# Diagonal and finest-level scores taken as channel sums, and two start-up slabs read in pairs

## The chip, the cores and the metric

The kernel runs on one core of one Trainium2 chip, as one launch. The metric is the device time of the launch in microseconds (us), the median of several runs. TensorE (PE in the profile) multiplies matrices, VectorE (DVE), ScalarE (ACT) and GpSimd (POOL) do the elementwise work, and SyncE (SP) issues nearly all DMAs. Each engine works through its own list of instructions in order, and semaphores are the only thing that holds one engine for another.

## The reference

One inference step of a one-layer decoder: 256 prompt tokens and 8 sample tokens share all weights, and everything is float32. A gated linear recurrence with twelve heads (eight HGRN2 heads with values 128 wide, four GLA heads with values 256 wide) stands between large projections.

```python
a = _rmsnorm(h, n_pre_mix)
z = einsum('bld,dn->bln', a, w_in)              # about 10,300 columns
o_h, s_h = _gated_recurrence(q_h, k_h, i_h, log_f, s_h0)
o_g, s_g = _gated_recurrence(q_g, k_g, v_g, log_a, s_g0)
merged = sigmoid(m_h) * (norm(o_h) * silu(zg) @ w_hgrn_up) + sigmoid(m_g) * (norm(o_g) * silu(gr) @ w_gla_up)
h = h + _rmsnorm(merged @ w_out, n_post_mix)
h = h + _rmsnorm(square(relu(_rmsnorm(h) @ w_ff1)) @ w_ff2, n_post_ffn)
h = h + sigmoid(h @ w_ple_gate) * (p_i @ w_ple)

# inside a block of the recurrence, b is the running sum of the log gates:
decay  = exp(where(causal, b[t] - b[s], -inf))
scores = einsum('bhtk,bhsk,bhtsk->bhts', q, k, decay)
o      = einsum('bhts,bhsv->bhtv', scores, v) + (q * exp(b)) @ state
```

For t = s the decay is 1, so that score is the sum over the 128 channels of q[t]·k[t].

## The kernel before, in words

Tokens lie along the free dimension (264 = 256 + 8), features along the 128 partitions. The weights lie in DRAM as tiles of 128 output features by 2048 inputs, in the order of use, and are read in halves, called slabs (128x1024, 512 KB), into a ring of four. A float32 product is made of three products in the rounded type fp32r: ACT rounds a slab (`round_slab`, line 355, raw to whi), DVE takes the remainder (`rest_slab`, line 360, wlo), and TensorE multiplies whi and wlo by the rounded activations and whi by their remainder (lines 380 to 382, 24 matmuls of 264 columns a slab). Each engine waits for the one ahead of it: SP for the remainder that frees a raw slot, ACT for the landing and for TensorE to have left the slot of whi, DVE for ACT, TensorE for DVE.

The first tile group (`T_RANK`) is eight tiles wide: for each of the 16 input blocks k, one slab holds this block of all eight tiles, 128 columns of each. Slabs k = 0 and 1 are read in two halves of four tiles each (lines 471 to 477), slabs 2 and on whole (line 348); all in pieces of 128 columns. Between them SP reads parts of the activations x.

The heads run in loops (first head alone, then heads 1 to 7, then 8 to 11), each over eight slabs of other projections, so that TensorE has work while the head's own chain passes through the other engines. On TensorE, after slab 4 of a head come: transposition of v (`turn_v`, line 757), the scores (`scores`, lines 761 to 771), transposition of the decayed keys (`turn_kd`, line 778); slabs 5 and 6; scores times v (`prob_v`, line 787) and the new state (line 795); slab 7, with the sum of squares for the head's norm in its middle (`head_norm`, lines 801 and 802 for the eight narrow heads, 805 for the four wide ones).

The scores are made by levels. Level 0 couples the two blocks of 128 tokens; level l = 1 to 7 couples the neighbouring halves of length 128 >> l, and the two diagonal blocks (line 766) hold the terms t = s. Each is a plain float32 matmul of 128 columns, which runs as two instructions. DVE makes the decays (`level_decays`), ACT takes their exponential, and DVE multiplies them by q and k (`level_operands`). After the scores DVE masks them from PSUM (lines 1581 and 1584) and adds the levels into three blocks, `pairs` (line 1592). Here `slab(n)` on DVE or ACT is the preparation of the slab that TensorE takes two later; on DVE the order after the last level is kd (1559), slab(4), slab(5), m_tile(1), slab(6), masks and additions, slab(7), m_tile(2), the first half of the next head's decays (1444 to 1447), then `sq_lo` (1603), the remainder of the squares that `head_norm` multiplies. POOL copies q and k of the next head (1937, 1939) once the scores of this head are done, and for the wide heads adds the squares of two tiles (1944).

Of the kernel before, what the change touches and what calls it, by code (L numbers as in the profile page):

```python
# [28 lines left out]
P = 128  # L29
# [72 lines left out]
def build(nc, t):  # L102
# [79 lines left out]
    with nc.sbuf_tensor("gate_w", [2 * RANK, GH * P], F32) as gate_w, nc.sbuf_tensor("rank_z", [2 * RANK, TOK], F32) as rank_z:  # L182
        pass
    S = sb("S", [P, 2, UNIT])
# [6 lines left out]
    with nc.sbuf_tensor("o_first", [P, TOK], F32), nc.sbuf_tensor("sq_lo", [P, NP_TOK], F32R) as sq_lo:  # L191
# [32 lines left out]
    first_landed = [sem(f"first_landed{k}") for k in range(HALVED)]  # L224
# [25 lines left out]
        "act": ["v_tok_ready", "lev_exp", "kd_exp", "kd_tok_ready", "sq_ready", "sq_rounded",  # L250
                "ln_rs", "rs_ready", "o_hi_done", "s_out_ready", "sg_abs", "sg_exp", "sg_ln", "sg_sigma"],
        "dve": ["sq_parted", "lev_sub", "lev_ready", "kd_ready", "masked", "probs_ready", "sg_ls",
# [63 lines left out]
    def lefts(ap, h):  # L316
        return cells(ap, h, 0, P + h, 2 * h)

# [22 lines left out]
    def load_wide(sp, T, k, tile, first=False):  # L341
# [3 lines left out]
        if not first:  # L345
            sp.wait_ge(lo_ready, 2 * T + (k - RING + 1))
# [14 lines left out]

    def rank_rest(dve, T, par, half, end, done):

        s = slot_of(par, half)
        hi = whi[:, s, 0:RANK].bitcast(F32)
        dve.tensor_tensor(whi[:, s, RANK:2 * RANK], raw[:, s, 0:RANK], hi, ALU.subtract)
        at = slice(P, end)
        dve.tensor_tensor(wlo[:, s, at], raw[:, s, at], whi[:, s, at].bitcast(F32), ALU.subtract).then_inc(done, 1)
# [95 lines left out]
    def _(sp):  # L464
# [6 lines left out]
        for k in range(HALVED):  # L471
            if k:
                load_x(k)
            for half, landed in enumerate((first_landed[k], slab_landed[k])):
                at = T_RANK + FIRST * half
                sp.dma_start(raw[:, k, part_of_first(half)].rearrange("p (n c) -> p n c", n=FIRST),
                             t["stream"][at:at + FIRST, :, k * P:(k + 1) * P].rearrange("n p c -> p n c")).then_inc(landed, 16)
        load_x(2)
        load_wide(sp, T_RANK, 2, T_RANK, first=True)
# [6 lines left out]
        for dst, name in ((masks, "masks"), (ident, "ident"), (head_gain, "head_gain"),  # L486
                          (gate_b, "gate_b")):
            sp.dma_start(dst[:], t[name]).then_inc(const_landed, 16)
        for part in range(2):
# [182 lines left out]
    def _(pe):  # L672
# [28 lines left out]
        pe.wait_ge(const_landed, 16 * 6)  # L701
# [59 lines left out]
        def scores(H, D):  # L761
            pe.wait_ge(h_sem["lev_ready"], now(H))
# [7 lines left out]
            pe.matmul(DG[:, P:2 * P], lev[:, 0, 1, :], lev[:, 0, 0, :], start=True, stop=True)\  # L770
              .then_inc(h_sem["scores_done"], 1)
# [9 lines left out]
        def prob_v(H, D):  # L781
# [3 lines left out]
            for d in range(D):  # L785
                v = slice(d * P, (d + 1) * P)
                pe.matmul(O[d][:, 0:2 * P], v_tok[:, 0, v], pairs[:, 0:2, :], start=True, stop=False, skip_group_check=True)  # L787
                mm = pe.matmul(O[d][:, P:2 * P], v_tok[:, 1, v], pairs[:, 2, :], start=False, stop=True, skip_group_check=True)  # L788
# [9 lines left out]
        def head_norm(H, D):  # L798
            if D == 1:
                pe.wait_ge(h_sem["sq_parted"], now(H))  # L800
# [6 lines left out]
        def head(H, D, first=False):  # L807
# [16 lines left out]
            turn_kd(H)  # L824
            slab(5)
# [111 lines left out]
    def _(act):  # L937
# [27 lines left out]
        for k in range(KT):  # L965
# [5 lines left out]
            if k < HALVED:  # L971
                act.wait_ge(first_landed[k], 16)
                act.copy(whi[:, k, part_of_first(0)], raw[:, k, part_of_first(0)]).then_inc(first_hi, 1)
                act.wait_ge(slab_landed[k], 16)
                act.copy(whi[:, k, part_of_first(1)], raw[:, k, part_of_first(1)]).then_inc(hi_ready, 1)
# [140 lines left out]
        def head(H, D, next_D, first=False):  # L1116
# [21 lines left out]
            slab(5)  # L1138
            slab(6)
            turned(H, D)  # L1140
# [10 lines left out]
            if D == 1:  # L1151
                act.wait_ge(h_sem["sq_ready"], now(H))
                act.copy(sq_hi[:], sq[:, 0, 0:NP_TOK]).then_inc(h_sem["sq_rounded"], 1)
# [173 lines left out]
    def _(dve):  # L1327
# [14 lines left out]
        for k in range(KT):  # L1342
# [5 lines left out]
            if k < HALVED:  # L1348
# [4 lines left out]
                dve.tensor_tensor(wlo[:, k, at], raw[:, k, at], whi[:, k, at].bitcast(F32), ALU.subtract)\  # L1353
# [133 lines left out]
        dve.wait_ge(const_landed, 16 * 6)  # L1487
# [27 lines left out]
        def head(H, D, more=True, opening=False):  # L1515
# [20 lines left out]
            def level_operands(l):  # L1536
# [16 lines left out]
            def last_levels():  # L1553
# [5 lines left out]
                dve.tensor_tensor(kd[:], kd[:], k_b[:, 0:NP_TOK], ALU.mult).then_inc(h_sem["kd_ready"], 1)  # L1559

# [10 lines left out]
            slab(4)  # L1571
            slab(5)
# [7 lines left out]
            for n, (first, last) in enumerate(((0, 4), (4, LEVELS - 1))):  # L1580
# [3 lines left out]
            dve.tensor_tensor(pairs[:], DG[:, 0:3 * P].rearrange("s (b t) -> s b t", b=3),  # L1584
                              ident[:].rearrange("s (b t) -> s b t", b=3), ALU.mult).then_inc(h_sem["masked"], 1)
            for l in range(1, LEVELS):
                h = HALF[l]
                to = cells(pairs[:, 0, :], h, h, 2 * P - h, 2 * h)
                of = packed(probs[:, l - 1, :], h)

                dve.wait_ge(h_sem["masked"], (LEVELS + 1) * H + (l + 3))
# [471 lines left out]
```

## Time and profile before

| | |
|---|---|
| median of 3 runs | 1628.47 us (1628.04 to 1629.47) |
| profiled execution, its own time | 1628.97 us |
| its span | 1627.2 us |
| PE busy | 1620.3 us (100%) in 13332 matmuls |
| DVE busy | 1109.9 us (68%) |
| ACT busy | 842.2 us (52%) |
| POOL busy | 181.7 us (11%) |
| DMA | 329.17 MB, mean 202 GB/s |
| granted TensorE clock | 1.00 throughout |

A matmul's duration in the trace (0.28 us for 264 columns) is its passage through the pipeline; the next one starts after about 0.12 us. What TensorE costs is therefore read from starts, not from durations. The heads lie between about 253 and 600 us of the span.

### The profile page before, as it was taken

Reading aid. Unit: us, or ns where it says so; the run is one execution under the profiler, and the core shown is the slowest. Engines: PE = TensorE matmul, PEld = TensorE weight load, DVE = VectorE, ACT = ScalarE, POOL = GpSimd, SP = SyncE. Lnnn points to the kernel's source line nnn. Section 1 sums busy time; section 2 is a strip of 40 time slices with the busy share of each in tenths; the row PEclk is TensorE's granted clock in tenths of the full one; section 3 lists DMA queues with packets and bytes.
Section 4 is the critical chain, followed back from the end, with each engine's and each line's share of the span. In section 5 each row is a group of like instructions: output and inputs, shape, how many; then the busy total and the mean of one; then the engine's idle time right before and its main releaser. Section 6 shows DMA issues by size and latency. Waiting matters only on the chain.

```text
span 1627.2 us, 35049 instructions
## 1 busy us (share of the span) xinstructions
PE 1620.3 (100%) x13332; PEld 1615.8 (99%) x13332; DVE 1109.9 (68%) x1917; ACT 842.2 (52%) x1192; POOL 181.7 (11%) x166
## 2 busy tenths in 40 slices
PE   9999999999999999999999999999999999999999
PEld 9999999999999999999999999999999999999999
DVE  7548767888888876655986665566555665555774
ACT  7575765666666665433654334443444334443452
POOL 3101000111111100055300000000000000035200
PEclk9999999999999999999999999999999999999999
DMA  9577895565555467755675865588557775555564
GB/s 274 161 230 225 267 270 174 164 191 162 192 166 181 155 206 229 270 181 185 173 214 186 247 207 180 188 259 243 174 181 242 245 222 185 181 197 181 167 192 144
DMA packets 151178, 329.17 MB, mean 202 GB/s; under 512 B 16944, under 2 KB 79536, under 8 KB 150608
## 3 DMA queue, kind: packets, MB, share of 16 engines
q1 hardware_dynamic: 143888, 326.00, 64.3%
q10 hardware_dynamic: 7232, 2.43, 0.6%
q8 instruction: 33, 0.54, 0.1%
q14 instruction: 25, 0.20, 0.0%
HBM read 310.08 MB, written 18.30 MB: 202 GB/s over the span
## 4 chain that ended last, share of the span: by engine, by line
PE 98%; DMA 1%; DVE 1%; ACT 0%; SPq 0%; issue 0%
PE bank L380 29%; PE bank L381 29%; PE bank L382 28%; PE bank L398 3%; PE bank L400 3%; PE bank L403 2%; PE bank L768 1%; DMA raw<-in_stream 1%; PE bank L795 0%; PE bank L787 0%; PE bank L766 0%; PE bank L788 0%; PE bank L757 0%; PE bank L732 0%; PE bank L770 0%; PE bank L778 0%
## 5 line engine op out<-in xcount | busy, mean ns | idle before, releaser
L355 ACT CAST whi<-raw 128x1024 fp32r<-128x1024 f32 x532 | 547.9, 1048 | 470.7 <-PE bank L382 388.5
L380 PE MATMUL bank<-a_hi,whi 128*128 128x264 f32 x2576 | 734.2, 285 | 0.1
L381 PE MATMUL bank<-a_hi,wlo 128*128 128x264 f32 x2576 | 729.7, 283 | 0.0
L382 PE MATMUL bank<-a_lo,whi 128*128 128x264 f32 x2576 | 729.4, 283 | 0.0
L360 DVE TENSOR_TENSOR wlo<-raw,whi 128x1024 fp32r<-128x1024 f32 x518 | 629.6, 1246 | 109.8 <-ACT whi L355 108.8
L380 PEld LDWEIGHTS bank<-a_hi,whi 128*128 128x128 f32 x2576 | 485.2, 188 | 0.8 <-issue 0.7
L381 PEld LDWEIGHTS bank<-a_hi,wlo 128*128 128x128 f32 x2576 | 485.5, 188 | 0.1
L382 PEld LDWEIGHTS bank<-a_lo,whi 128*128 128x128 f32 x2576 | 482.9, 187 | 0.0
L380 PE MATMUL bank<-b_hi,whi 128*128 128x264 f32 x1280 | 363.1, 284 | 0.0
L381 PE MATMUL bank<-b_hi,wlo 128*128 128x264 f32 x1280 | 362.6, 283 | 0.0
L382 PE MATMUL bank<-b_lo,whi 128*128 128x264 f32 x1280 | 362.4, 283 | 0.0
L381 PEld LDWEIGHTS bank<-b_hi,wlo 128*128 128x128 f32 x1280 | 241.2, 188 | 0.0
L380 PEld LDWEIGHTS bank<-b_hi,whi 128*128 128x128 f32 x1280 | 241.1, 188 | 0.0
L382 PEld LDWEIGHTS bank<-b_lo,whi 128*128 128x128 f32 x1280 | 239.9, 187 | 0.0
L1281 ACT ACTIVATE lev<-lev 128x264 f32<-128x264 f32 x64 | 27.2, 425 | 165.5 <-DVE lev L1777 165.5
L1690 DVE TENSOR_TENSOR room<-room,bank 128x264 f32<-128x264 f32 (+1 forms) x48 | 20.6, 429 | 106.9 <-PE bank L382 106.9
L1883 POOL TENSOR_TENSOR sq<-room 128x264 f32<-128x264 f32 x2 | 2.2, 1086 | 721.9 <-DVE room L1690 620.0
L398 PE MATMUL bank<-b_hi,whi 128*128 128x264 f32 x256 | 73.3, 286 | 0.3 <-DVE b_lo L1339 0.3
L403 PE MATMUL bank<-b_hi,wlo 128*128 128x264 f32 x256 | 72.8, 284 | 0.0
L400 PE MATMUL bank<-b_lo,whi 128*128 128x264 f32 x256 | 72.7, 284 | 0.0
L1783 DVE TENSOR_TENSOR a_lo<-lev,a_hi 128x264 f32 (+1 forms) x64 | 27.3, 432 | 63.8 <-ACT a_hi L1283 63.8
L1777 DVE SCALAR_TENSOR_TENSOR lev<-bank,r_bc 128x264 f32<-128x264 f32 x64 | 27.1, 432 | 52.6 <-PE bank L382 52.5
(222 smaller groups left out, 1497.7 us busy)
## 6 DMA issues: line engine op xcount, KB each, us to landing
raw<-in_stream SPq DMA_DIRECT2D x532, 512.0 KB, 4.7
m_spill<-stage SPq DMA_DIRECT2D x32, 132.0 KB, 3.7
lev<-m_spill SPq DMA_DIRECT2D x16, 264.0 KB, 2.8
room<-in_x SPq DMA_DIRECT2D x7, 528.0 KB, 7.8
S<-in_state_hgrn SPq DMA_DIRECT2D x6, 512.0 KB, 6.7
out_new_hgrn_sample<-S SPq DMA_DIRECT2D x6, 512.0 KB, 6.8
S<-in_state_gla SPq DMA_DIRECT2D x5, 512.0 KB, 6.7
out_new_gla_sample<-S SPq DMA_DIRECT2D x5, 512.0 KB, 7.5
```

Source lines behind the costliest of these rows:

```text
L355: act.copy(whi[:, s, :], raw[:, s, :]).then_inc(hi_ready, 1)
L360: dve.tensor_tensor(wlo[:, s, :], raw[:, s, :], whi[:, s, :].bitcast(F32), ALU.subtract).then_inc(lo_ready, 1)
L380: pe.matmul(out, whi[:, s, w], hi[:, k0 + k, :], start=start and k == 0, stop=False)
L381: pe.matmul(out, wlo[:, s, w], hi[:, k0 + k, :], start=False, stop=False)
L382: mm = pe.matmul(out, whi[:, s, w], lo[:, k0 + k, :], start=False, stop=stop and k == HT - 1)
L398: pe.matmul(out, whi[:, s, w], hi[:, k, :], start=k == 0, stop=False, skip_group_check=True)
L400: mm = pe.matmul(out, whi[:, s, w], lo[:, k, :], start=False, stop=rank and k == KT - 1, skip_group_check=True)
L403: return pe.matmul(out, wlo[:, s, w], hi[:, k, :], start=False, stop=k == KT - 1, skip_group_check=True)
L1281: act.activation(u, u, ACT.Square).then_inc(u_ready, 1)
L1690: ins = dve.tensor_tensor(out, out, MM[par][:, 0:TOK], ALU.add)
L1777: dve.scalar_tensor_tensor(out=u, in0=bank[:, 0:TOK], scalar=0.0, in1=r_bc[:], op0=ALU.max, op1=ALU.mult).then_inc(tiles_drained, 1)
L1783: dve.tensor_tensor(a_lo[:, T - T0, :], u, a_hi[:, T - T0, :].bitcast(F32), ALU.subtract).then_inc(a_lo_ready, 1)
```

## The change

In each head the two diagonal matmuls and the one of level 7 go. Instead three rows of products are summed over the channels by TensorE with a matrix of ones: q·k of the two blocks, made on POOL (`dots_of`), and the product of the two operands of level 7, made on DVE, in a tile `dots` of 384 columns. ACT rounds it to `dots_hi`, DVE takes the remainder `dots_lo`, and two fp32r matmuls of 384 columns (`sum_dots`) follow the transposition of kd. ACT copies v and rounds `dots` ahead of its slab(6); DVE moves slab(6) behind the masks and additions. The mask of the last level becomes an instruction of its own. At the start, slabs 1 and 2 of the first tile group are read together: four tiles of both in one DMA, in pieces of 256 columns (1024 bytes), then the other four; the second part of x follows them. `ident` is read in three DMAs with its blocks in another order.

```diff
@@ sync: first loads
-        for k in range(HALVED):
-            if k:
-                load_x(k)
-            for half, landed in enumerate((first_landed[k], slab_landed[k])):
-                at = T_RANK + FIRST * half
-                sp.dma_start(raw[:, k, part_of_first(half)]..., t["stream"][at:at + FIRST, :, k * P:(k + 1) * P]...)
+        for half, landed in enumerate((first_landed, slab_landed[0])):
+            at = T_RANK + FIRST * half
+            sp.dma_start(by_block(raw[:, 0, part_of_first(half)]), t["stream"][at:at + FIRST, :, 0:P]...).then_inc(landed, 16)
+        load_x(1)
+        for half in range(2):
+            at = T_RANK + FIRST * half
+            sp.dma_start(raw[:, 1 + half, :]..., t["stream"][at:at + FIRST, :, P:3 * P]...).then_inc(slab_landed[1 + half], 16)
         load_x(2)
-        load_wide(sp, T_RANK, 2, T_RANK, first=True)
         load_wide(sp, T_RANK, 3, T_RANK, first=True)
@@ load_wide
-            sp.wait_ge(lo_ready, 2 * T + (k - RING + 1))
+            sp.wait_ge(lo_ready, 2 * T + (k - RING + (2 if T == T_RANK and k == RING + 1 else 1)))
@@ tensor: scores
-            for B in range(2):
-                at = slice(B * P, (B + 1) * P)
-                pe.matmul(DG[:, 2 * B * P:(2 * B + 1) * P], k_b[:, at], q_b[:, at], start=True, stop=True)
-            for l in range(1, LEVELS):
+            for l in range(1, LEVELS - 1):
...
+        def sum_dots(H, D):
+            pe.wait_ge(h_sem["parts_ready"], dots_now(H, D))
+            pe.matmul(DG[:, 0:3 * P], ones_r[:], dots_hi[:], start=True, stop=False)
+            pe.matmul(DG[:, 0:3 * P], ones_r[:], dots_lo[:], start=False, stop=True).then_inc(h_sem["scores_done"], 1)
@@ tensor: head
             turn_kd(H)
+            sum_dots(H, D)
             slab(5)
@@ scalar: head
             slab(5)
+            turned(H, D)
+            act.wait_ge(h_sem["kq_ready"], second_now(H))
+            act.wait_ge(h_sem["lev_ready"], second_now(H))
+            act.copy(dots_hi[:], dots[:]).then_inc(h_sem["parts_rounded"], 1)
             slab(6)
-            turned(H, D)
@@ vector: last_levels
+                dve.wait_ge(h_sem["lev_ready"], first_now(H))
+                dve.tensor_tensor(dots[:, 0:P], lev[:, LEVELS - 1, 0, :], lev[:, LEVELS - 1, 1, :], ALU.mult)
@@ vector: head
             slab(4)
+            dve.wait_ge(h_sem["parts_rounded"], dots_now(H, D))
+            dve.tensor_tensor(dots_lo[:], dots[:], dots_hi[:].bitcast(F32), ALU.subtract).then_inc(h_sem["parts_ready"], 1)
             slab(5)
...
-            slab(6)
             dve.wait_ge(h_sem["scores_done"], now(H))
...
+            dve.tensor_tensor(probs[:, LEVELS - 2, :], DG[:, 0:P], both[:, LEVELS - 2, :], ALU.mult).then_inc(h_sem["masked"], 1)
...
+            slab(6)
@@ gpsimd
+        def dots_of(H):
+            pool.wait_ge(h_sem["kq_ready"], first_now(H))
+            pool.tensor_tensor(turned_blocks(dots), q_b[:, 0:NP_TOK]..., k_b[:, 0:NP_TOK]..., ALU.mult).then_inc(h_sem["kq_ready"], 1)
```

On TensorE, in the loop of heads 1 to 7, the stretch from the transposition of v to slab 5 was:

```order
L757 MATMUL bank<-ident,v_st 128x128
L762 REGISTER_ALU
L766 MATMUL bank<-q_b,k_b 128x128 [waits ln_rs,lev_ready]
L766 MATMUL bank<-q_b,k_b 128x128
L768 MATMUL bank<-lev,k_lev 128x128 x7
L770 MATMUL bank<-lev 128x128
L778 MATMUL bank<-ident,kd 128x128 [waits v_tok_ready,kd_ready]
```

The same stretch is now the following, with other line numbers (797 for 768, 811 for 778):

```order
L789 MATMUL bank<-ident,v_st 128x128
L794 ISA
L797 MATMUL bank<-lev,k_lev 128x128 [waits ln_rs,lev_ready]
L797 MATMUL bank<-lev,k_lev 128x128 x5
L799 MATMUL bank<-lev 128x128
L808 REGISTER_ALU
L811 MATMUL bank<-ident,kd 128x128 [waits v_tok_ready,kd_ready]
L811 MATMUL bank<-ident,kd 128x128
L803 MATMUL bank<-dots_hi,ones_r 128x384 [waits parts_ready]
L804 MATMUL bank<-dots_lo,ones_r 128x384
```

Three float32 matmuls are gone, and two of 384 columns stand behind the transposition of kd with a wait of their own.

On DVE, in the same loop, from kd to the mask of the diagonal blocks, before (L360 is the remainder of a slab, L1373 the drain m_tile(1)):

```order
L1559 TENSOR_TENSOR kd<-kd,k_b 128x256 [waits kd_exp]
L359 ISA
L360 TENSOR_TENSOR wlo<-raw,whi 128x1024 [waits hi_ready]
L359 REGISTER_ALU
L360 TENSOR_TENSOR wlo<-raw,whi 128x1024 [waits hi_ready]
L1373 TENSOR_TENSOR stage<-bank,r_bc 128x264 [waits slabs_multiplied]
L359 ISA
L360 TENSOR_TENSOR wlo<-raw,whi 128x1024 [waits hi_ready]
L1579 REGISTER_ALU [waits scores_done]
L1581 TENSOR_TENSOR probs<-bank,both 128x512 [waits pv_done]
L1581 TENSOR_TENSOR probs<-bank,both 128x384
L1584 TENSOR_TENSOR pairs<-bank,ident 128x384
```

And now (L380 is the remainder, L1412 the drain):

```order
L1600 TENSOR_TENSOR kd<-kd,k_b 128x256 [waits kd_exp]
L1602 TENSOR_TENSOR dots<-lev 128x128 [waits lev_ready]
L380 TENSOR_TENSOR wlo<-raw,whi 128x1024 [waits hi_ready]
L1616 TENSOR_TENSOR dots_lo<-dots,dots_hi 128x384 [waits parts_rounded]
L379 REGISTER_ALU
L380 TENSOR_TENSOR wlo<-raw,whi 128x1024 [waits hi_ready]
L1412 TENSOR_TENSOR stage<-bank,r_bc 128x264 [waits slabs_multiplied]
L1623 REGISTER_ALU [waits scores_done]
L1625 TENSOR_TENSOR probs<-bank,both 128x512 [waits pv_done]
L1625 TENSOR_TENSOR probs<-bank,both 128x256
L1628 TENSOR_TENSOR probs<-bank,both 128x128
L1629 TENSOR_TENSOR pairs<-bank,ident 128x384
```

`dots` and `dots_lo` have come in, the third remainder has moved behind the additions, and the second mask is in two pieces.

On SP, the first loads were (in_x are parts of x, in_stream are slabs):

```order
L476 DMA raw<-in_stream 128x4x128 x2
L467 DMA room<-in_x 128x264
L476 DMA raw<-in_stream 128x4x128 x2
L467 DMA room<-in_x 128x528
L348 DMA raw<-in_stream 128x8x128 x2
```

They are now:

```order
L503 DMA raw<-in_stream 128x4x128 x2
L497 DMA room<-in_x 128x264
L508 DMA raw<-in_stream 128x4x256 x2
L497 DMA room<-in_x 128x528
L368 DMA raw<-in_stream 128x8x128
```

Slab 2 has moved ahead of the part of x that holds k = 2 and 3, and the halves of slab 1 come with those of slab 2.

## Rows read from the trace of the kernel before

**Rows 1.** The page's chain of work that ended last, shares of the span.
```profile
PE 98%; DMA 1%; DVE 1%; ACT 0%; SPq 0%; issue 0%
```

**Rows 2.** Timeline of PE in head 3: start, duration, engine, line, operation, count.
```profile
349.84 0.38 PE L757 MATMUL bank<-ident,v_st 128*128 128x128 f32 x2
350.06 0.61 PE L766 MATMUL bank<-q_b,k_b 128*128 128x128 f32 x4
350.51 1.73 PE L768 MATMUL bank<-lev,k_lev 128*128 128x128 f32 x14
352.30 0.38 PE L778 MATMUL bank<-ident,kd 128*128 128x128 f32 x2
...
361.58 0.28 PE L801 MATMUL bank<-sq_hi,ones_r 128*128 128x256 f32 x1
361.70 0.28 PE L802 MATMUL bank<-sq_lo,ones_r 128*128 128x256 f32 x1
```

**Rows 3.** Timeline of DVE in head 3, from kd to sq_lo.
```profile
349.43 0.41 DVE L1559 TENSOR_TENSOR kd<-kd,k_b 128x256 f32<-128x256 f32 x1
349.77 2.35 DVE L360 TENSOR_TENSOR wlo<-raw,whi 128x1024 fp32r<-128x1024 f32 x2
...
358.80 0.28 DVE L1444 TENSOR_TENSOR lev<-cum 128x128 f32<-128x128 f32 x1
...
360.41 0.42 DVE L1603 TENSOR_TENSOR sq_lo<-sq,sq_hi 128x256 fp32r<-128x256 f32 x1
```

**Rows 4.** Timeline of ACT in head 3.
```profile
351.00 0.37 ACT L1096 COPY v_tok<-bank 128x256 f32<-128x256 f32 x1
```

**Rows 5.** Timeline of DVE in the first tile group.
```profile
8.84 0.55 DVE L368 TENSOR_TENSOR wlo<-raw,whi 128x384 fp32r<-128x384 f32 x1
9.31 0.68 DVE L1353 TENSOR_TENSOR wlo<-raw,whi 128x512 fp32r<-128x512 f32 x1
...
12.78 1.08 DVE L368 TENSOR_TENSOR wlo<-raw,whi 128x896 fp32r<-128x896 f32 x1
```

**Rows 6.** Timeline of PE in the first tile group; brackets: idle time, releaser.
```profile
14.01 0.36 PE L398 MATMUL bank<-a_hi,whi 128*128 128x264 f32 x1 [0.91 <-DVE wlo L368]
...
23.00 0.36 PE L398 MATMUL bank<-a_hi,whi 128*128 128x264 f32 x1 [0.23 <-DVE wlo L368]
```

**Rows 7.** Timeline of ACT in the first tile group.
```profile
8.60 0.62 ACT L975 CAST whi<-raw 128x512 fp32r<-128x512 f32 x1
...
9.84 0.89 ACT L969 ACTIVATE a_hi<-room,gains 128x128 fp32r<-128x128 f32 x3 [0.29 <-DMA room<-in_x]
11.61 1.05 ACT L355 CAST whi<-raw 128x1024 fp32r<-128x1024 f32 x1 [0.88 <-DMA raw<-in_stream]
```

**Rows 8.** Timeline of PE in head 9 (a wide head).
```profile
514.58 0.60 PE L757 MATMUL bank<-ident,v_st 128*128 128x128 f32 x4
515.03 0.38 PE L766 MATMUL bank<-q_b,k_b 128*128 128x128 f32 x1
...
527.01 0.59 PE L805 MATMUL bank<-sq,ones 128*128 128x256 f32 x2
```

**Rows 9.** Timeline of DVE in head 9.
```profile
514.89 0.42 DVE L1559 TENSOR_TENSOR kd<-kd,k_b 128x256 f32<-128x256 f32 x1
```

**Rows 10.** What PE waited for ahead of line 766: releaser, us, times.
```profile
  DVE k_lev L1544: 0.2, 1
```

**Rows 11.** Timeline of PE between heads 0 and 1.
```profile
285.99 0.28 PE L382 MATMUL bank<-a_lo,whi 128*128 128x264 f32 x1
286.38 0.38 PE L380 MATMUL bank<-a_hi,whi 128*128 128x264 f32 x1
```

**Rows 12.** Timeline of POOL: the squares of head 9, and a product during two remainders.
```profile
525.64 0.91 POOL L1944 TENSOR_TENSOR sq<-sq 128x256 f32<-128x256 f32 x1 [5.99 <-ACT sq L1149]
...
691.69 1.54 POOL L1885 TENSOR_TENSOR sq<-room 128x264 f32<-128x264 f32 x1 [5.17 <-DVE room L1692]
```

**Rows 13.** Timeline of DVE during that product.
```profile
691.52 2.78 DVE L360 TENSOR_TENSOR wlo<-raw,whi 128x1024 fp32r<-128x1024 f32 x2
```

More of the change, by code:

```diff
@@ L183, in build @@
         pass
+    with nc.sbuf_tensor("dots", [P, 3 * P], F32) as dots, nc.sbuf_tensor("dots_hi", [P, 3 * P], F32R) as dots_hi, \
+         nc.sbuf_tensor("dots_lo", [P, 3 * P], F32R) as dots_lo:
+        pass
     S = sb("S", [P, 2, UNIT])
@@ L223, in build @@
     gains_landed = sem("gains_landed")
-    first_landed = [sem(f"first_landed{k}") for k in range(HALVED)]
+    first_landed = sem("first_landed")
     first_hi, first_lo = sem("first_hi"), sem("first_lo")
@@ L307, in before, with dots_now, first_now, second_now @@
         return H + 1
+    def dots_now(H, D):
+        return 2 * H + 2 if D == 1 else H + (HH + 2)
+    def first_now(H):
+        return 2 * H + 2
+    def second_now(H):
+        return 2 * H + 3
     def cells(ap, h, at, step, pitch):
@@ L317, in lefts, with turned_blocks @@
         return cells(ap, h, 0, P + h, 2 * h)
+    def turned_blocks(dots):
+        ap = dots[:, 2 * P:3 * P]
+        return bass.AP(ap.tensor, ap.offset, [list(ap.ap[0]), [-P, 2], [1, P]])
     def packed(ap, h):
@@ L360, in rest_slab, with by_block, first_rows @@
         dve.tensor_tensor(wlo[:, s, :], raw[:, s, :], whi[:, s, :].bitcast(F32), ALU.subtract).then_inc(lo_ready, 1)
+    def by_block(ap):
+        return ap.rearrange("p (n c) -> p n c", c=P)
+    def first_rows(k):
+        if k in (1, 2):
+            return raw[:, 1:3, :].rearrange("p s (n b c) -> p (s n) b c", n=FIRST, b=2)[:, :, k - 1, :]
+        return by_block(raw[:, k % RING, :])
     def rank_rest(dve, T, par, half, end, done):
-        s = slot_of(par, half)
+        s, k = slot_of(par, half), 2 * T + half
         hi = whi[:, s, 0:RANK].bitcast(F32)
-        dve.tensor_tensor(whi[:, s, RANK:2 * RANK], raw[:, s, 0:RANK], hi, ALU.subtract)
+        dve.tensor_tensor(whi[:, s, RANK:2 * RANK], first_rows(k)[:, 0, 0:RANK], hi, ALU.subtract)
         at = slice(P, end)
-        dve.tensor_tensor(wlo[:, s, at], raw[:, s, at], whi[:, s, at].bitcast(F32), ALU.subtract).then_inc(done, 1)
+        dve.tensor_tensor(by_block(wlo[:, s, at]), first_rows(k)[:, 1:end // P, :], by_block(whi[:, s, at].bitcast(F32)), ALU.subtract)\
+           .then_inc(done, 1)
     def multiply(pe, T, par, half, out, hi, lo, k0, start, stop, before_k=None, midway=None, at=HT // 2):
@@ L485, in _ @@
                 load_x(4 + (k - RING) // 3)
-        for dst, name in ((masks, "masks"), (ident, "ident"), (head_gain, "head_gain"),
-                          (gate_b, "gate_b")):
+        for dst, name in ((masks, "masks"), (head_gain, "head_gain"), (gate_b, "gate_b")):
             sp.dma_start(dst[:], t[name]).then_inc(const_landed, 16)
+        for to, of in ((0, 0), (1, 2), (2, 1)):
+            sp.dma_start(ident[:, to * P:(to + 1) * P], t["ident"][:, of * P:(of + 1) * P]).then_inc(const_landed, 16)
         for part in range(2):
@@ L799, in head_norm @@
             if D == 1:
-                pe.wait_ge(h_sem["sq_parted"], now(H))
+                pe.wait_ge(h_sem["parts_ready"], second_now(H))
                 pe.matmul(DG[:, 0:NP_TOK], ones_r[:], sq_hi[:], start=True, stop=False)
@@ L1601, in head @@
             if D == 1:
-                dve.wait_ge(h_sem["sq_rounded"], now(H))
-                dve.tensor_tensor(sq_lo[:], sq[:, 0, 0:NP_TOK], sq_hi[:].bitcast(F32), ALU.subtract).then_inc(h_sem["sq_parted"], 1)
+                dve.wait_ge(h_sem["parts_rounded"], second_now(H))
+                dve.tensor_tensor(sq_lo[:], sq[:, 0, 0:NP_TOK], sq_hi[:].bitcast(F32), ALU.subtract).then_inc(h_sem["parts_ready"], 1)
             slab(8)
@@ L1956, in _ @@
         pool.tensor_copy(by_head(s_cols[:, 3, :, :]), gates[:, :, at]).then_inc(cols_ready, 1)
+        pool.wait_ge(units_summed, HEADS)
+        with pool.Fori(0, 1) as H:
+            dots_of(H)
         with pool.Fori(1, HH) as H:
             head(H, 1)
+            dots_of(H)
         with pool.Fori(HH, HH + 1) as H:
             head(H, 2)
+            dots_of(H)
         with pool.Fori(HH, HEADS - 1) as H:
             head(H + 1, 2)
+            dots_of(H + 1)
             add_halves(H)
```

54 lines of the change are left out of this document (31 added, 23 removed).

## The prediction

> **What bounds the kernel now.** I read the page's chain of waits first: 98% of the span is TensorE, one matmul behind another [rows 1]. So an edit counts only by what it does to TensorE's list: work taken out of it, put into it, or a wait. The list of waits by engine names no stall of TensorE in the heads longer than 0.2 us, so I went on to the timelines of a steady narrow head (head 3), engine by engine, with t = 0 at the first transposition of v, 349.84 [rows 2], and looked for how early each partner is. All times below are after that zero.
>
> TensorE: scores from 0.22, kd's transposition at 2.46, head_norm at 11.74 [rows 2]. DVE begins kd at -0.41 and then shows no idle time down to sq_lo, which ends at 10.99 [rows 3]: all these 11 us it is one unbroken list. TensorE starts a matmul 0.15 us after the end of the remainder it waited for (12.78 + 1.08 = 13.86 against 14.01) [rows 5, 6]. DVE is thus 11.74 - 10.99 - 0.15 = 0.60 us early for head_norm, and the change puts work into just this stretch.
>
> **The change, part by part.** *Matmuls.* From 350.51 to 352.30 pass 14 instructions of line 768 and the two of line 770: 1.79 / 16 = 0.112 us each [rows 2]. Six go per head (two diagonals and level 7, two instructions each): 0.67 us. Two fp32r matmuls of 384 columns come in. The trace has 256 columns, 0.12 us from start to start [rows 2]. Between 0.12 (no dearer) and 0.18 (in proportion to the columns) I take 0.17, near proportion, since most of the 0.12 is columns. That adds 0.34. Net -0.33 us a head, -4.0 us for twelve, if nothing waits. The Trainium skill (TensorE: Matmul & The Clock Gate, section Back-to-back issue gap) gives a gap that grows with the columns plus a few ns; by it a matmul would be 0.16 us and the gain 0.2 us larger in all.
>
> *DVE's list* grows by three things: dots, 128 columns, 0.20 (eight such instructions between 358.80 and 360.41) [rows 3]; dots_lo, 384 columns, 0.47 (8.84 to 9.31) [rows 5]; the mask cut in two, another start, about 0.07 (what 0.20 for 128 and 0.47 for 384 columns leave for no columns). Together 0.74 us. slab(6) only changes places within the list, between kd and sq_lo both before and now, and frees nothing there. Behind dots_lo stand slab(5), m_tile(1), the masks and all the rest.
>
> *Where that ends.* If DVE starts where it does now, sq_lo comes 0.74 later and TensorE asks for it 0.33 earlier: 1.07 less the 0.60 in hand, a stall of 0.47 at head_norm. A stall gives DVE a longer lead into the next head, but the lead can't be used, since dots_lo waits for ACT: the transpositions end at 0.38 [rows 2], ACT's copy of v takes 0.37 [rows 4], of which the next instruction overlaps some 0.1, and the rounding of 384 columns about 0.5 (512 columns took 0.62 [rows 7]). So dots_hi ends near 1.21 and dots_lo starts near 1.24. From the end of the first remainder of rows 3 (1.14, half of 2.35 less the overlap) to the end of sq_lo DVE needs 10.99 - (-0.07) - 1.14 = 9.92; with dots_lo and the cut mask 10.46. That is 11.70, plus 0.15 for the hand-over 11.85, against TensorE at 11.41: a stall of 0.44. The two ways agree; I take 0.45. The first matmul after a wait took 0.36 instead of 0.28 [rows 2, 6], so 0.08 more. The wait of sum_dots itself costs nothing here: dots_lo ends at 1.79, seen at 1.94, and TensorE arrives at 2.46 - 0.67 + 0.13 = 1.92. A steady narrow head is then -0.33 + 0.45 + 0.08 = +0.20; heads 0 and 2 to 7: +1.4.
>
> *Between heads 0 and 1* TensorE has a gap of 0.39 instead of 0.12 [rows 11], behind a chain that starts at scores times v of head 0; a stall ahead of it is absorbed there: -0.27.
>
> *Late heads.* In head 9 DVE starts kd 0.31 after TensorE's transpositions begin, 0.72 later than in head 3 [rows 8, 9]. There kd 0.34, dots 0.20 and the remainder 1.14 put dots_lo at 1.99, its end at 2.54, seen at 2.69. TensorE, starting scores at 0.45 [rows 8], is there at 0.45 + 14 x 0.112 + 0.14 = 2.16: a stall of 0.53, and +0.20 net. Heads 10 and 11 look the same in the trace. The wide heads have no sq_lo. +0.6 for three. Head 8 is early, but its copy of v is twice as wide: a stall of about 0.2, -0.1 net. Head 1 is the one in which TensorE waited for DVE's last level [rows 10]: a late head that also has sq_lo, +0.6.
>
> *POOL's product* lies behind the copies of q and k for the next head, 20 us before it is wanted. While it runs DVE masks from PSUM. I cost it at nothing; if DVE were held by it, about 0.4 us a head would come on top (the hold in rows 13).
>
> *Start.* The pair lands before the second part of x. ACT met slab 1 already there at 8.60, x at 9.84 and slab 2 at 11.61 [rows 7]: 512 KB in about 1.77 us. Without faster pieces slab 1's second half comes near 10.4, x not after 11.6, ACT reaches slab 2 about 0.9 later and TensorE starts it at 14.9 instead of 14.01 [rows 6]. If pieces of 1024 bytes save a fifth of 3.5 us for the pair, it is 14.2. The second wait, 23.00, is behind a slab that comes after all these bytes and not later than before; it ends the start-up either way, and swallows a delay of up to about 0.4 us. I take -0.1, between -0.5 and +0.5. The three reads of ident and SP's two more issues, at 29 us, stand in a stretch where nothing on TensorE waits.
>
> Sum: 1.4 - 0.27 + 0.6 - 0.1 + 0.6 - 0.1 = +2.1 us. Against the profiled execution, 1628.97, that is 1631.1; the median of the runs is 0.5 lower, so the forecast is **1630.6 us**.
>
> **Rivals.** *No stalls: the gain is whole.* -4.0 - 0.1 gives 1624.4 us. For it: no listed wait in the heads now, and DVE has idle time in other stretches. Against: the 0.60 us at head_norm is measured, and 1.07 goes into it. *Half stalls*, where dots and dots_lo cost DVE or ACT less than the nearest rows say, or TensorE resumes faster: 0.2 us instead of 0.53 in seven heads, -2.3, near 1628 us. *POOL's squares are shut out (slower).* In the wide heads head_norm waits for POOL's sum of squares (line 1944), 525.64 in head 9, 11.06 after its zero, needed at 12.43 [rows 8, 12]. DVE now runs the next head's decays from about 10.4 to 12.1 and slab(8) straight behind them to 13.3. If POOL can't get in between, its sum ends near 13.9, and TensorE, due at 12.6, stands 1.4 us, in heads 8 to 10 (the last has no decays): +4.3, 1635 us. It decides as soon as slab(8) is ready before the decays end, which by my times is so by 0.1 us. Against it: at 691.69 POOL's product came during one remainder and was done before the second [rows 12], and the two together took 2.78 instead of 2.35 [rows 3, 13], so POOL got in between them at DVE's cost. By the Trainium skill (SBUF — State Buffer, section Who interferes with whom) a DVE instruction with two SBUF inputs and a POOL read contend, and the one issued first holds the port to its end; by that POOL waits one instruction and this rival falls. The rows just named agree, 0.43 us.
>
> **How the numbers follow.** The forecast has 0.52, its own range 1628.9 to 1632.9 (0.15 us up or down in ten heads, the start). Half stalls 0.22, no stalls 0.11, POOL shut out 0.15. No change that this measurement can tell is 0.2%, 1625.2 to 1631.7. Faster: the first rival, 0.11. Slower: the last rival and a fifth of the forecast's chance, 0.26. Within: 0.63. The range for 8 in 10, 1626.5 to 1634.0, leaves out most of the two outer rivals.
>
> **What would show it.** In the new profile: matmuls of 384 columns 0.16 to 0.18 us apart, and six fewer of 0.11; TensorE waiting for sq_lo at head_norm in the narrow heads by 0.3 to 0.6 us, DVE's list unbroken from dots_lo to sq_lo; sum_dots waiting for dots_lo in heads 1 and 9 to 11 by about 0.5 and hardly in heads 2 to 7; POOL's squares done before line 805's matmuls are due. At the start the wait for slab 2 shifts, and the sixth slab still starts near 23. Wrong would be: no wait at head_norm (then it is faster), stalls over 1 us in the wide heads (then slower), or a start-up that ends later than 23.5.

## The result, and the profile after

The changed kernel takes 1633.03 us (median of 12 runs, 1632.24 to 1636.41), the one before 1628.72 us beside it (12 runs, 1628.04 to 1629.47). The ratio is 1.0029, 95% interval 1.0021 to 1.0036: slower by 0.29%, 4.3 us. That lies inside the range (1626.5 to 1634.0) and 2.4 us above the forecast of 1630.6; the case thought likeliest, no change that can be told, did not come, since the whole interval is above 0.2%.

The page's first line of busy times and its chain of waits, to be held against [rows 1]:

```profile
PE 1620.2 (99%) x13284; PEld 1612.3 (99%) x13284; DVE 1120.7 (69%) x1953; ACT 848.0 (52%) x1204; POOL 181.3 (11%) x178
PE 89%; DVE 5%; issue 3%; ACT 1%; DMA 1%; POOL 1%; SPq 0%; DVEq 0%; ACTq 0%; POOLq 0%
```

TensorE has 48 matmuls less, and the span is 4.2 us longer (1631.4 against 1627.2): no work was added to TensorE, it waits. For what, the list of waits says (engine, line, releaser: us in total, times, longest; the two rows left out, of 1.7 and 0.3 us, are in the kernel before too). Of the rows shown, the kernel before has only the first kind:

```profile
PE bank L398 <- DVE wlo L368: 1.1, 2, 0.9
```

The changed kernel:

```profile
PE bank L428 <- DVE wlo L397: 2.4, 2, 1.5
...
PE bank L834 <- DVE sq_lo L1649: 1.3, 7, 0.2
PE bank L838 <- POOL sq L1996: 1.3, 1, 1.3
...
PE bank L803 <- DVE dots_lo L1616: 0.2, 1, 0.2
```

The first is the start-up, the second the norm of the narrow heads, the third the norm of a wide head, the fourth `sum_dots`. The next table is made from starts of matmuls in the two traces, in us: for each head the start of its first transposition of v, and the period to the next head's.

```
head   start before/after   period before/after  more   forecast
0      265.08  266.11       30.107  30.180      +0.07   -0.07 (with the gap behind it)
1      295.18  296.29       27.447  27.987      +0.54   +0.6
2..7   322.63  324.27       27.207  27.346      +0.14   +0.20   (each; six heads)
8      485.88  488.34       28.700  29.014      +0.31   -0.1
9      514.58  517.35       28.827  30.333      +1.51   +0.20
10     543.40  547.68       28.814  29.014      +0.20   +0.20
11     572.22  576.70       (to its norm)       -0.31   +0.20
```

Head 0 starts 1.03 late, the start-up's share (forecast -0.1). The heads add 3.14 (forecast 2.2). Behind them nothing is gained or lost.

**The start-up.** ACT's timeline (start, duration, instruction, in brackets the idle time before it and its releaser), then TensorE's; they answer to [rows 6, 7]:

```profile
9.96 0.62 ACT L1007 CAST whi<-raw 128x512 fp32r<-128x512 f32 x1 [1.74 <-DMA raw<-in_stream]
11.46 0.62 ACT L1009 CAST whi<-raw 128x512 fp32r<-128x512 f32 x1 [0.88 <-DMA raw<-in_stream]
...
13.09 1.03 ACT L1011 CAST whi<-raw 128x1024 fp32r<-128x1024 f32 x1
```

```profile
11.40 0.36 PE L428 MATMUL bank<-a_hi,whi 128*128 128x264 f32 x1 [1.55 <-DVE wlo L397]
...
15.48 0.36 PE L428 MATMUL bank<-a_hi,whi 128*128 128x264 f32 x1 [0.89 <-DVE wlo L397]
```

Slab 1's second half, rounded at 8.60 before, is in at 11.46. Slab 2 came with it, but ACT reaches its rounding only at 13.09, behind that half and the next part of x. TensorE stands twice before 16 us, and slab 2, the third slab, starts at 15.48 instead of 14.01. The wait that ended at 23.00 before is gone and gives 0.4 back.

**A steady narrow head.** TensorE at `sum_dots` and at the norm in head 3 (its zero is 351.62), then DVE; they answer to [rows 2, 3]:

```profile
353.40 0.38 PE L811 MATMUL bank<-ident,kd 128*128 128x128 f32 x2
353.54 0.42 PE L803 MATMUL bank<-dots_hi,ones_r 128*128 128x384 f32 x1
353.80 0.34 PE L804 MATMUL bank<-dots_lo,ones_r 128*128 128x384 f32 x1
353.98 0.28 PE L410 MATMUL bank<-a_hi,whi 128*128 128x264 f32 x1
354.09 0.28 PE L411 MATMUL bank<-a_hi,wlo 128*128 128x264 f32 x1
...
362.93 0.29 PE L412 MATMUL bank<-a_lo,whi 128*128 128x264 f32 x1
363.39 0.39 PE L834 MATMUL bank<-sq_hi,ones_r 128*128 128x256 f32 x1 [0.17 <-DVE sq_lo L1649]
363.61 0.28 PE L835 MATMUL bank<-sq_lo,ones_r 128*128 128x256 f32 x1
```

```profile
352.85 0.56 DVE L1616 TENSOR_TENSOR dots_lo<-dots,dots_hi 128x384 fp32r<-128x384 f32 x1 [0.33 <-ACT dots_hi L1178]
...
362.91 0.42 DVE L1649 TENSOR_TENSOR sq_lo<-sq,sq_hi 128x256 fp32r<-128x256 f32 x1
```

`sum_dots` does not wait. The norm starts 0.46 after the matmul ahead of it instead of 0.12 and its second matmul 0.22 after the first instead of 0.12: 0.34 of waiting and 0.10 of starting again.

**A wide head.** Head 9 on POOL, DVE and TensorE (the POOL row of before is in [rows 12], the norm in [rows 8]):

```profile
528.40 2.74 POOL L1996 TENSOR_TENSOR sq<-sq 128x256 f32<-128x256 f32 x1 [6.00 <-ACT sq L1188]
```

```profile
528.93 0.28 DVE L1485 TENSOR_TENSOR lev<-cum 128x128 f32<-128x128 f32 x1
529.13 0.29 DVE L1486 TENSOR_TENSOR lev<-cum 128x128 f32<-128x128 f32 x1
529.34 1.22 DVE L380 TENSOR_TENSOR wlo<-raw,whi 128x1024 fp32r<-128x1024 f32 x1
```

```profile
531.19 0.70 PE L838 MATMUL bank<-sq,ones 128*128 128x256 f32 x2 [1.26 <-POOL sq L1996]
```

POOL's sum of the squares, 0.91 us before, takes 2.74: it is asked for amid DVE's decays, which follow each other without a gap, and the remainder of slab(8) starts before the last of them has ended. It ends 0.58 after that remainder, and TensorE has stood 1.4 us. In heads 8 and 10 the same sum takes 1.60:

```profile
499.21 1.60 POOL L1996 TENSOR_TENSOR sq<-sq 128x256 f32<-128x256 f32 x1 [6.01 <-ACT sq L1188]
...
558.55 1.60 POOL L1996 TENSOR_TENSOR sq<-sq 128x256 f32<-128x256 f32 x1 [6.01 <-ACT sq L1188]
...
587.48 0.74 POOL L1996 TENSOR_TENSOR sq<-sq 128x256 f32<-128x256 f32 x1 [27.33 <-ACT sq L1188]
```

There it got through before the remainder was done (which took 1.75 instead of 1.22), and TensorE lost 0.27 by waiting and 0.10 by starting again. Head 11, without decays, takes 0.74.

### The profile page after: what moved, and what is told of

It reads as the page before. It is cut to its first block, busy times and chain, and to the rows that moved or that the text cites. A ratio compares the mean times of both kernels' runs of the same rounds, so it can differ in the third digit from the quotient of the medians.

```text
span 1631.4 us, 35080 instructions
## 1 busy us (share of the span) xinstructions
PE 1620.2 (99%) x13284; PEld 1612.3 (99%) x13284; DVE 1120.7 (69%) x1953; ACT 848.0 (52%) x1204; POOL 181.3 (11%) x178
## 4 chain that ended last, share of the span: by engine, by line
PE 89%; DVE 5%; issue 3%; ACT 1%; DMA 1%; POOL 1%; SPq 0%; DVEq 0%; ACTq 0%; POOLq 0%
PE bank L411 26%; PE bank L410 26%; PE bank L412 26%; PE bank L428 3%; PE bank L430 3%; PE bank L433 3%; DVE wlo L380 1%; DMA raw<-in_stream 1%; DVE pairs L1637 1%; DVE probs L1625 0%; POOL sq L1996 0%; ACT whi L375 0%; DVE lev L1485 0%; DVE lev L1486 0%; PE bank L797 0%
## 5 line engine op out<-in xcount | busy, mean ns | idle before, releaser
L380 DVE TENSOR_TENSOR wlo<-raw,whi 128x1024 fp32r<-128x1024 f32 x518 | 631.4, 1250 | 101.4 <-ACT whi L375 100.1
```

The source lines that it names most:

```text
L380: dve.tensor_tensor(wlo[:, s, :], raw[:, s, :], whi[:, s, :].bitcast(F32), ALU.subtract).then_inc(lo_ready, 1)
```

## The experiments

Each kernel was timed in five rounds beside the kernel before on the same chip; all ratios are to it.

**Start-up of before (heads_only).** The changed kernel with the old loads:

```diff
+        for k in range(HALVED):
+            if k:
+                load_x(k)
+            for half, landed in enumerate((first_landed[k], slab_landed[k])):
...
         load_x(2)
+        load_wide(sp, T_RANK, 2, T_RANK, first=True)
```

> The changed kernel with the start-up loads of the kernel before (slabs 1 and 2 apart, the second part of x ahead of slab 2); the heads are the changed ones. Theory: the paired start-up costs 1.0 us, as the two profiles have it (the gates' matmuls at 61.6 instead of 60.6), because slab 1's second half lands behind slab 2's first: 1632.0 us, 1.0 less than the changed kernel; the first wait ends near 14.0 again and the sixth slab's near 23.0. Rival: the 1.0 us is chance in when the first loads arrive (the first product started 0.4 us apart in the two profiles): 1633.0 us.

1631.33 us, ratio 1.0020 (1.0010 to 1.0029), 1.5 us less than the change by the ratios. All head periods from head 1 on are those of the changed kernel within 0.02 us; head 0's is 0.37 shorter, since `sum_dots` does not wait there. The wait for slab 2 ends at 13.80, and none follows.

**Pair alone (start_only).** The reverse, the paired loads in the kernel before:

```diff
+        load_x(1)
+        for half in range(2):
+            at = T_RANK + FIRST * half
+            sp.dma_start(raw[:, 1 + half, :]..., t["stream"][at:at + FIRST, :, P:3 * P]...)
         load_x(2)
-        load_wide(sp, T_RANK, 2, T_RANK, first=True)
```

> The kernel before with the paired start-up alone; its heads are those of before. Theory: the pair costs what its removal gave back, ratio 1.0020 instead of 1.0029, some 1.4 us, whatever the heads are: 1629.6 us, ratio 1.0008; head 0 starts near 266 instead of 265.1. Rival: the delay is taken up before the heads, by waits that the kernel before has anyway: ratio 1.000.

1629.60 us, ratio 1.0008 (0.9999 to 1.0017); its trace has the two waits, at 11.37 (1.70 us) and 15.45 (0.89), and every head starts 1.0 late with an unchanged period. Over all profiles here, head 0 starts at 265.41 to 266.25 in five kernels with the pair in 1024-byte pieces and at 264.21 to 265.24 in four with the old loads, 1.2 us apart in the mean, and the two groups do not overlap. So the pair costs 1.0 to 1.5 us, whatever the heads are; that it costs anything is shown by the profiles, since the interval of start_only alone reaches no change.

**Pieces of 512 bytes (packets_512).** The order of the pair, not its pieces:

```diff
-            sp.dma_start(raw[:, 1 + half, :]..., t["stream"][at:at + FIRST, :, P:3 * P]...)
+            for k in (1, 2):
+                sp.dma_start(raw[:, 1 + half, :]...[:, :, k - 1, :], t["stream"][at:at + FIRST, :, k * P:(k + 1) * P]...)
```

> The changed kernel with the pair of slabs read in the same order and into the same places, but in four transfers with pieces of 512 bytes instead of two with pieces of 1024. Theory: the order alone (half of slab 2 ahead of slab 1's second half) makes the start-up late and the size of the pieces does nothing: 1633.0 us, the third slab near 15.5. Rival: pieces of 1024 bytes do save time, a fifth of the pair's 3.5 us, and the order's cost is larger than it looks: about 0.7 us later at the third slab, 1633.7 us.

1633.09 us, ratio 1.0028 (1.0018 to 1.0039): the time of the change, but in the profile it is made up otherwise. ACT's rounding of slab 1's second half and of slab 2, TensorE's start on slab 2, and its wait for POOL:

```profile
10.41 0.62 ACT L1010 CAST whi<-raw 128x512 fp32r<-128x512 f32 x1 [1.14 <-DMA raw<-in_stream]
...
12.04 1.03 ACT L1012 CAST whi<-raw 128x1024 fp32r<-128x1024 f32 x1
```

```profile
14.43 0.36 PE L428 MATMUL bank<-a_hi,whi 128*128 128x264 f32 x1 [0.89 <-DVE wlo L397]
```

```profile
PE bank L839 <- POOL sq L1997: 2.5, 2, 1.3
```

Slab 2 starts at 14.43, where the five kernels with large pieces have 14.78 to 15.48, and head 0 at 265.05, below all five (265.41 to 266.25) and among those with the old loads. The same total comes about because POOL holds up heads 9 and 10 here (periods +1.51 and +1.35 against before), where the change's profile has head 9 alone (head 10 +0.20). So neither theory is borne out, and the equal times do not show that the order makes the whole cost: in this one profiled execution head 0 starts 0.4 to 1.2 us earlier than with large pieces in the same order. How the cost divides between the order and the pieces stays open.

**Slab 2 ahead of x, without the pair (x_behind).** The kernel before with two lines exchanged:

```diff
-        load_x(2)
         load_wide(sp, T_RANK, 2, T_RANK, first=True)
+        load_x(2)
```

> The kernel before with one thing of the paired start-up: slab 2 is read ahead of the second part of x, in pieces of 512 bytes; slab 1 is not joined with it. Theory: the start-up's cost is that slab 1's second half waits for the first half of slab 2 (the wait of 1.97 us at the second slab); without the pair this wait isn't there, x comes some 1.8 us later than before, slab 2 starts near 14.9 instead of 14.0, and the wait near 22.5 takes up half of that: +0.4 us, ratio 1.0002. Rival: x behind slab 2 is the whole cost (the third slab waits for ACT, which waits for x), as much as with the pair: ratio 1.0008.

1630.25 us, ratio 1.0007 (0.9998 to 1.0016), as much as the pair by the ratio; but it does not tell the theories apart, since something else came in. TensorE's wait for slab 2 is one of 1.89 us, the third slab starts at 14.26 (0.25 later than before, less than either theory had), and no later wait is left; yet head 0 starts 1.33 late. The table by windows (stretch, its length, PE busy and matmuls, granted clock, DMA share, GB/s) shows why:

```profile
12.00:14.00 2.00, 0.37 (x4) 1.00 1.08 344
14.00:16.00 2.00, 1.74 (x13) 0.89 1.09 351
16.00:18.00 2.00, 2.00 (x11) 0.50 1.16 311
18.00:20.00 2.00, 2.00 (x14) 0.76 1.19 295
```

Behind that single wait the granted clock fell to half, 1.2 GHz, and came back before 20 us: 1.33 - 0.25 + 0.4 (the later wait that is gone) = some 1.5 us. In the profiles of the changed kernel and of the pair alone, where the idle time comes in two parts of 1.55 to 1.70 and 0.89 us, the clock is 1.00 in these stretches. Of the eleven timed runs of x_behind five have a mean clock of 0.999 (median 1630.55 us) and six 1.000 (median 1629.29, 0.8 above before), so the fall does not come every time. What x's place alone costs stays open.

**sq_lo ahead of the decays (sq_early).**

```diff
+            if D == 1:
+                dve.wait_ge(h_sem["parts_rounded"], second_now(H))
+                dve.tensor_tensor(sq_lo[:], sq[:, 0, 0:NP_TOK], ...)
             if more:
                 dve.wait_ge(h_sem["cum_ready"], now(H + 1))
                 level_half(0)
-            if D == 1:
...
```

> The changed kernel with sq_lo, the remainder that the narrow heads' norm waits for, ahead of the next head's first decays on DVE instead of behind them. Theory: TensorE waits at the norm because DVE's list ahead of sq_lo grew by 0.7 us, while its input has been ready for 1.4 us: the wait goes in heads 1 to 7, 0.37 us each, 2.6 us in all, near 1630.4 us, and a narrow head's period falls from 27.34 to 26.98. Rival 1: the input from ACT is what comes late, and nothing changes (1633.0). Rival 2: the decays, now 0.4 us later, delay the next head, and the wait comes back at sum_dots or at the scores: 1632 to 1633 us.

1629.47 us, ratio 1.0004 (0.9995 to 1.0013). The wait is gone in all seven heads, and a steady period is 26.90 instead of 27.35, 0.31 shorter than before the change (forecast 26.98; the 0.10 of starting again goes with the wait). Head 3:

```profile
360.68 0.42 DVE L1646 TENSOR_TENSOR sq_lo<-sq,sq_hi 128x256 fp32r<-128x256 f32 x1
```

```profile
362.10 0.29 PE L412 MATMUL bank<-a_lo,whi 128*128 128x264 f32 x1
362.22 0.28 PE L834 MATMUL bank<-sq_hi,ones_r 128*128 128x256 f32 x1
362.34 0.28 PE L835 MATMUL bank<-sq_lo,ones_r 128*128 128x256 f32 x1
```

The first theory holds; the decays, 0.4 later, delay nobody in heads 1 to 6, and head 7 by 0.1. In this profile heads 9 and 10 both wait 1.4 us for POOL, where the change's own had that in head 9 alone; the profiled execution, 1631.28 us, is the slowest of the eleven.

**Decays behind slab(8) in the wide heads (wide_order).**

```diff
-            if more:
+            if more and D == 1:
                 dve.wait_ge(h_sem["cum_ready"], now(H + 1))
                 level_half(0)
...
             slab(8)
+            if more and D == 2:
+                dve.wait_ge(h_sem["cum_ready"], now(H + 1))
+                level_half(0)
```

> The changed kernel with, in the wide heads 8 to 11, the next head's first decays behind slab(8) on DVE instead of ahead of it, which leaves DVE idle for about 1.4 us when the squares of the head come. Theory: POOL's sum of squares (1.60, 2.74 and 1.60 us in heads 8 to 10, 0.74 in head 11 that has no decays) is held out by DVE's decays and the remainder right behind them; without them it takes 0.74 to 0.9 us, and the waits at the norm go: 0.37 + 1.51 + 0.37 us less, near 1630.8 us. Rival: POOL's sum is long for another reason (its two inputs in one tile, ACT's reads), the waits stay: 1633.0 us. A second rival: the decays, 1.3 us later, make ACT's exponential and the next head's scores late: slower than 1633 us.

1630.78 us, ratio 1.0018 (1.0009 to 1.0027). POOL's sum in head 9, and where DVE's remainder now stands:

```profile
526.95 0.75 POOL L1999 TENSOR_TENSOR sq<-sq 128x256 f32<-128x256 f32 x1 [5.54 <-ACT sq L1188]
```

```profile
527.84 1.23 DVE L380 TENSOR_TENSOR wlo<-raw,whi 128x1024 fp32r<-128x1024 f32 x1 [1.47 <-ACT whi L375]
528.98 0.28 DVE L1483 TENSOR_TENSOR lev<-cum 128x128 f32<-128x128 f32 x1
```

The sum takes 0.75 us in all four wide heads, and the norm waits in none; heads 8 and 9 are 0.37 and 1.49 shorter. Of this 0.2 to 0.3 comes back in heads 10 and 11, where `sum_dots` waits again for `dots_lo`: the stall of head 9 had given DVE a lead.

**Diagonals alone (diag_only).** Level 7 stays a matmul of its own:

```diff
-            for l in range(1, LEVELS - 1):
+            for l in range(1, LEVELS):
...
-            pe.matmul(DG[:, 0:3 * P], ones_r[:], dots_hi[:], start=True, stop=False)
+            pe.matmul(DG[:, P:3 * P], ones_r[:], dots_hi[:, P:3 * P], start=True, stop=False)
```

> The changed kernel with level 7 as before: its matmul with the other levels, its mask with theirs, no product of it on DVE. Only the two diagonal blocks are summed over the channels (256 columns), and the rest of the change, paired start-up too, stays. Theory: the wait at the norm in the narrow heads is DVE's added 0.74 us less the 0.60 in hand and the matmuls saved; here DVE gets only 0.34 (256 columns) and TensorE loses four matmuls of 0.112 for two of some 0.14: sq_lo is 0.1 early, the wait is gone, a narrow head is 0.17 shorter than before, and with the start-up's 1.4 us the whole is near that of before, 1628.5, ratio 1.000. Rival: the wait comes from ACT's detour (the copy of v and the rounding ahead of its slab(6), which is there in both), and stays: ratio 1.002.

1629.47 us, ratio 1.0006 (0.9997 to 1.0015), between the theory's 1.000 and the rival's 1.002. In heads 2, 4, 6 and 7 the norm no longer waits and the period is 0.15 to 0.18 shorter than before; in heads 3 and 5 it waits 0.12 and the period is 0.03 to 0.04 longer; head 1 waits 0.24. This fits the length of DVE's list, to within a tenth. By itself it does not clear ACT's detour, which is shorter too (it rounds 256 columns instead of 384); sq_early does, where ACT's detour is that of the change and the wait is gone all the same. What I had not expected of it is POOL: its sum takes 1.44, 2.79 and 1.44 us in heads 8 to 10, and head 9 stands 1.5 us, with the smaller change too.

**The three corrections together (best), and without level 7 (best_diag).** The edits of heads_only, sq_early and wide_order in one kernel; then those of diag_only as well.

> The changed heads with three things put right: the start-up loads of the kernel before, sq_lo ahead of the next head's decays in the narrow heads, and in the wide heads the decays behind slab(8). Theory: the three costs are apart from each other, so the head periods of the single runs add up: against the kernel before -0.3 in head 0, +0.05 in head 1, -0.31 in each of heads 2 to 6, -0.2 in head 7, about 0 in heads 8 to 11, no start-up cost: -2.0 us, ratio 0.9988 (1626.2 us where the kernel before has 1628.2). Rival: DVE's list has no slack left, what is moved back delays the next head's scores or sum_dots, and half of it is lost: ratio 0.9995.

> The corrected version (start-up of before, sq_lo early, decays behind slab(8) in wide heads) with level 7 left as before, so that only the diagonal blocks are channel sums. Theory: a narrow head saves 4 x 0.112 - 2 x 0.12 = 0.21 us instead of 0.31, but in the late heads 1 and 9 to 11 sum_dots no longer waits for dots_lo, which is 0.1 us shorter with two instructions less in front of it, worth 0.25 to 0.3 us each: -0.2 in eight heads, -0.25 in four, -2.6 us in all against -2.0 for the version with level 7; ratio 0.9984. Rival: what the late heads win at sum_dots they wait at the next hand-over (the drains on DVE): -1.8 us, ratio 0.9989, not better than the version with level 7.

best: 1626.57 us, ratio 0.9991 (0.9982 to 1.0000). The periods of its heads 0 to 10 add up to -2.0 us against before, as forecast: -0.27, +0.02, five times -0.31, -0.24, and within 0.06 of nothing in heads 8 to 10. The saving of the wide heads is lost at `sum_dots`, which waits there for `dots_lo`. best_diag: 1625.88 us, ratio 0.9984 (0.9975 to 0.9993), faster than both kernels. All its heads are 0.17 to 0.25 shorter than before, 2.4 us in all against the 2.6 forecast, and of TensorE's waits only those of the start-up and one of 0.3 us behind the heads, which all kernels have, are left:

```profile
PE bank L724 <- POOL eps_col L1913: 1.7, 1, 1.7
PE bank L426 <- DVE wlo L395: 1.1, 1, 1.1
PE bank L426 <- DVE b_lo L1372: 0.3, 1, 0.3
```

That it beats best is likely but not shown: 0.7 us in the medians, on two chips, and the intervals overlap. It gains per late head what best loses, 0.2, and loses 0.1 per narrow head.

## Why the prediction was right and where it was wrong

**The start-up was mis-sized, with the wrong sign: -0.1 forecast, +1.0 in the profile, 1.3 to 1.5 by the timed pairs of kernels.** The step that failed is "slab 1's second half comes near 10.4"; it came at 11.46, where half of slab 2 goes with its first half, ahead of it. That this order alone makes it late is not shown: with pieces of 512 bytes in the same order the half was rounded at 10.41, as forecast (packets_512, one profile). ACT's serial list made it worse: the half, a part of x, and only then slab 2, 1.48 us later than before and not 0.9. And the second wait was not an end that swallows a delay: it was 0.39 long, gave that back, and went. By 1.47 - 0.39 = 1.08 the profile's 1.03 is accounted for. I had written that a start-up ending later than 23.5 would prove me wrong; the sixth slab, by which I dated that end, starts at 24.08 instead of 23.00, so by its own sign this part was wrong; TensorE's last wait of the start-up now ends at 15.48.

**POOL's squares were shut out in one head of three.** I had this as a rival (0.15, 1.4 us in each of heads 8 to 10), with the right place and price. I gave it little because the rows of two remainders [rows 12, 13] showed POOL getting in between them. In head 9 it did not get in between decays and remainder, in heads 8 and 10 it did; the decays ended 1.0 us after it was asked for. The forecast had put all three heads on one side, and the condition that I gave the rival, slab(8) ready before the decays end, did not divide them either: the rounding ended 0.15 to 0.17 us before the last decay did in all three. With the page cited there (the Trainium skill, SBUF — State Buffer, section Who interferes with whom), by which the first issued holds the shared port to its end, POOL would have waited one decay of 0.28 us; here it waited for five in a row, the running one and four more, and in head 9 for the remainder too. The rule names the two engines rightly; that POOL gets in at the next boundary was my reading of it, and in an unbroken row it did not. wide_order shows that DVE's unbroken row is the cause. So it is not semaphores alone that hold one engine for another, as the section on the chip has it: no semaphore stands between this sum and the decays.

**The narrow heads were right, step by step.** Matmuls: from the transposition of kd to the second matmul of slab 5 pass 354.09 - 353.40 = 0.69 us; in the kernel before 0.34:

```profile
352.30 0.38 PE L778 MATMUL bank<-ident,kd 128*128 128x128 f32 x2
352.43 0.37 PE L380 MATMUL bank<-a_hi,whi 128*128 128x264 f32 x1
352.64 0.28 PE L381 MATMUL bank<-a_hi,wlo 128*128 128x264 f32 x1
```

So two matmuls of 384 columns cost 0.35, as priced (0.34), and the first fp32r matmul behind a float32 one costs 0.08 to 0.09 more in both kernels. The page cited there (the Trainium skill, TensorE: Matmul & The Clock Gate, section Back-to-back issue gap) would have 0.16 for one by itself; 353.80 to 353.98 is 0.18, and the measurement decides. Without stalls the period fell by 0.31 (sq_early), forecast 0.33. DVE: `dots_lo` starts 1.23 after the head's zero (forecast 1.24), and `sq_lo` ends at 11.71 (11.70). Only the hand-over was smaller: the norm starts 0.06 after `sq_lo` ends, not 0.15, so the wait was 0.34 instead of 0.45, and a steady head cost 0.14 instead of 0.20.

**The late heads were right in kind.** Head 1 +0.54 (0.6). Head 9 waits about 0.4 at `sum_dots` (0.53), heads 8, 10 and 11 about 0.2; 10 and 11 less than forecast, because of the lead that head 9's stall gave DVE (without that stall, in wide_order, both wait 0.34). Head 10's +0.20 is the forecast's by luck: 0.2 at `sum_dots` and 0.37 at the norm stand there for 0.53 at `sum_dots`. The gap between heads 0 and 1 did not take up anything (0.39 still): head 0's norm did not wait, so nothing was there to take up. In head 0 `sum_dots` waited 0.34 in the changed kernel's profile and not at all in those of heads_only and wide_order; why is open.

In sum, forecast +2.1 and measured +4.2 in the profiles: start-up +1.1, head 9 +1.3, head 8 +0.4, head 0 +0.1; against that heads 2 to 7 -0.4, head 11 -0.5, head 1 -0.1. The two terms that were wrong, the start-up and POOL's sum in heads 8 and 9, come to +2.9 and the others to -0.8; the time lies in the range because the range was wide enough to hold both misses.

## What to carry to other kernels

Work that leaves a saturated engine lands on another one's list: before moving it, find in that list the instruction that the first engine waits for next, and put that one ahead of what nobody wants yet (here `sq_lo` ahead of the decays, 0.45 us a head). When two transfers are joined, ask when the earlier slab's last byte comes, and not when the pair is done. A gap in DVE's list can be the time in which POOL's instruction gets through (0.75 us in wide_order, 1.60 or 2.74 without the gap); where such a gap goes, count that instruction as late.

## What the runs showed of the hardware

- POOL's sum of 256 columns took 0.74 us with DVE idle, 1.44 to 1.60 when it had to wait for a row of DVE decays, and 2.74 to 2.79 when the remainder behind them came first as well. Which of the two it was went with hundredths. In the four profiles with decays ahead of the remainder and all three sums (changed, heads_only, sq_early, packets_512), it began 77 to 83 ns after a decay in the six cases of 1.59 to 1.60, and 50 to 70 ns after one in the six of 2.74 to 2.76. The rounding of slab(8) ended 69 to 79 ns before the remainder began in the former and 82 to 102 ns in the latter, so the traces do not say which of the two decides. In diag_only the 1.44 came where DVE stood still for about 0.04 us ahead of the remainder, the 2.79 where it did not.
- The changed kernel, with pieces of 1024 bytes, moved some 7% more in the same stretch than packets_512, not the fifth that I had allowed for, and without any time won. Windows of the kernel before, the changed one and packets_512, in this order (granted clock, DMA share and GB/s last):

```profile
7.00:10.00 3.00, 2.94 (x23) 1.00 1.03 318
10.00:12.00 2.00, 2.00 (x19) 1.00 1.16 301
```

```profile
7.00:10.00 3.00, 2.85 (x24) 1.00 1.03 349
10.00:12.00 2.00, 0.60 (x5) 1.00 1.18 345
```

```profile
7.00:10.00 3.00, 2.63 (x22) 1.00 1.15 320
10.00:12.00 2.00, 1.77 (x12) 1.00 1.15 330
```

- One idle stretch of 1.89 us in the start-up was followed by half the clock; 1.70 and 0.89 us, one behind the other, were not, in the profiles of x_behind and start_only. In the timed runs the mean clock was below 1.000 in five of eleven and in one of eleven.
